# Output projection of an encoder layer as seven block products, with weight sums made in device memory and the second norm in two token halves

## What is computed

```python
mix = jnp.concatenate([o_att, o_hg], axis=-1) @ w_out[l]      # (512 x 2048) @ (2048 x 2048)
x = x + g1 * rms_norm(mix, norm_mix_post[l])
h = rms_norm(x, norm_ffn_pre[l]) * (1.0 + sc2) + sh2
y = conv_glu_ffn(h, w_up[l], conv_w[l], conv_b[l], w_down[l])  # starts with h @ w_up
```

## Time and profile before

| | us |
|---|---|
| median of 3 runs (lowest, highest) | 2378.76 (2375.49, 2380.01) |
| span of the profiled execution, from first to last instruction | 2375.8 |
| busy in it: PE / PEld / DVE / ACT / POOL | 2334.7 / 2025.8 / 1878.8 / 1104.8 / 128.6 |
| mean granted clock of TensorE | 0.997 |

### The profile page before, as it was taken

The page is one execution under the profiler, slowest core; times in us unless marked ns, Lnnn a source line. Parts: engine busy times, 40 slices in busy tenths (PEclk is TensorE's granted clock), DMA queues, the critical chain, the costliest instruction groups (busy, mean ns, idle before and its releaser), DMA issues.

```text
span 2375.8 us, 37218 instructions
## 1 busy us (share of the span) xinstructions
PE 2334.7 (98%) x13671; PEld 2025.8 (85%) x13671; DVE 1878.8 (79%) x2447; ACT 1104.8 (47%) x1517; POOL 128.6 (5%) x207
## 2 busy tenths in 40 slices
PE   6999999999999999999999999999999999999998
PEld 3577778888888877878999999999999998888887
DVE  5875667887777873267799999999999998888777
ACT  4266744334443353254444444444444445555554
POOL 1010000000000000000000000000000000001100
PEclk9999999999999999999999999999999999999999
DMA  9952456666666734336555555555555559779966
GB/s 366 346 157 85 133 180 208 215 219 212 207 211 198 234 89 169 98 124 159 146 140 146 145 144 143 144 142 139 141 145 145 142 176 329 251 207 285 279 226 224
DMA packets 378834, 442.47 MB, mean 186 GB/s; under 512 B 14876, under 2 KB 295716, under 8 KB 376448
## 3 DMA queue, kind: packets, MB, share of 16 engines
q1 hardware_dynamic: 359056, 369.74, 49.1%
q0 software_dynamic: 19696, 71.68, 13.0%
HBM read 418.81 MB, written 66.08 MB: 204 GB/s over the span
## 4 chain that ended last, share of the span: by engine, by line
PE 87%; DVE 5%; DMA 3%; ACT 2%; issue 2%; SPq 0%; DVEq 0%; ACTq 0%
PE bank L2132 26%; PE bank L2134 26%; PE bank L2133 26%; DMA ADA<-in_w_ada_dram 2%; PE bank L2295 2%; DVE ACC L1373 2%; DMA AB_raw<-in_w_ada_dram 1%; PE bank L2198 1%; DVE ZZ L1577 1%; PE bank L2375 1%; PE bank L2314 1%; PE bank L2189 1%; DVE W_lo L1332 0%; PE bank L2063 0%; DVE AB_acc L1636 0%
## 5 line engine op out<-in xcount | busy, mean ns | idle before, releaser
L2132 PE MATMUL bank<-H_lo,W_hi 128*128 128x256 f32 (+1 forms) x1832 | 635.7, 347 | 0.0
L2134 PE MATMUL bank<-H_hi,W_lo 128*128 128x256 f32 (+1 forms) x1832 | 613.6, 335 | 0.0
L2133 PE MATMUL bank<-H_hi,W_hi 128*128 128x256 f32 (+1 forms) x1832 | 613.2, 335 | 0.0
L2132 PEld LDWEIGHTS bank<-H_lo,W_hi 128*128 128x128 f32 x1832 | 349.3, 191 | 35.8 <-issue 6.2
L2133 PEld LDWEIGHTS bank<-H_hi,W_hi 128*128 128x128 f32 x1832 | 349.3, 191 | 35.7 <-issue 6.2
L2134 PEld LDWEIGHTS bank<-H_hi,W_lo 128*128 128x128 f32 x1832 | 348.8, 190 | 35.6
L2132 PE MATMUL bank<-T_lo,W_hi 128*128 128x256 f32 x1280 | 362.2, 283 | 0.0
L2133 PE MATMUL bank<-MGR,W_hi 128*128 128x256 f32 x1280 | 362.2, 283 | 0.0
L2134 PE MATMUL bank<-MGR,W_lo 128*128 128x256 f32 x1280 | 362.2, 283 | 0.0
L2132 PEld LDWEIGHTS bank<-T_lo,W_hi 128*128 128x128 f32 x1280 | 245.8, 192 | 0.0
L2133 PEld LDWEIGHTS bank<-MGR,W_hi 128*128 128x128 f32 x1280 | 245.8, 192 | 0.0
(11 more groups left out here) (311 smaller groups left out, 3741.7 us busy)
## 6 DMA issues: line engine op xcount, KB each, us to landing
AB_raw<-in_w_ada_dram SPq DMA_DIRECT2D x128, 512.0 KB, 4.4
UB<-in_w_up_dram SPq DMA_DIRECT2D x100, 512.0 KB, 4.1
W_raw<-in_w_in_dram SPq DMA_DIRECT2D x90, 512.0 KB, 4.8
t_dram<-in_w_down_dram POOLq DMA_DIRECT2D x88, 512.0 KB, 8.1
DRAW<-in_w_down_dram SPq DMA_DIRECT2D x66, 512.0 KB, 5.8
W_raw<-in_w_up_dram SPq DMA_DIRECT2D x56, 512.0 KB, 3.9
ADA<-in_w_ada_dram SPq DMA_DIRECT2D x48, 512.0 KB, 9.0
W_raw<-in_w_down_dram SPq DMA_DIRECT2D x44, 512.0 KB, 6.1
```

The source lines that it names most:

```text
L2132: pe.matmul(acc, st_hi, mv_lo, start=start, stop=False, skip_group_check=on)
L2133: pe.matmul(acc, st_hi, mv_hi, start=False, stop=False, skip_group_check=on)
L2134: return pe.matmul(acc, st_lo, mv_hi, start=False, stop=stop, skip_group_check=on)
```

## The change

**Seven products.** The projection is computed in 2 x 2 blocks: the 512 tokens in two halves, the 2048 rows of `w_out` in two halves of 1024, its columns in two halves of 1024. Seven products of (256 tokens x 1024) by (1024 x 1024) take the place of eight. Each has 8 units (128 rows of a weight or weight sum by 1024 columns), so there are 56 units of four steps (two token tiles by two column halves), 224 steps in all. The order is the list `OUT`. Four products need sums or differences of blocks of `MX`: DVE makes them in place (`combine`), and the parts go to `CH` and `CL` (four slots each of 8 rows by 256 tokens). Four banks (`CHAIN_A`) carry products 1, 6, 5, 3, 2 on top of each other, four (`CHAIN_C`) 7, 4 and, after a copy of product 1 back into them, 2; ACT keeps states (`keep_chain`), DVE adds them.

**Weight sums.** The products 7, 6, 5 and 4 use sums of blocks of `w_out`. POOL makes them in device memory (`out_sum`, 56 transfers of 512 KB): 16 copies beside the rotations of attention, 16 adds, 8 copies and 8 adds beside the heads, one for every two units, and 8 adds after `GROW` is loaded. SP waits for the last 8 ahead of product 4. The 22 copies of `w_down` move from the heads into the loop over the channel sub-layer (`sum_t2`, three for every two tiles).

**Last head.** `OUT_STEPS` now leaves out 4 of the first 56 steps instead of 8; 60 steps (15 units) lie in the last head. The gates are transposed at step 71.

**Norm in halves.** The right token half (tiles 2 and 3) is done after product 3, and its norm, its transposes (`turn_h2`, 16 turns of two transposes) and its splits lie beside product 2. The 30 matmuls without use go. `up_row` runs 16 times for the right half and 16 times for the left (256 columns each instead of 512).

```diff
+OUT = ([(1, k) for k in range(8)] + [(6, k) for k in range(7)] + [(7, 0), (6, 7), (7, 1)] + [(5, k) for k in range(8)]
+       + [(7, k) for k in range(2, 8)] + [(3, 0), (3, 1)] + [(4, k) for k in range(8)] + [(3, k) for k in range(2, 8)]
+       + [(2, k) for k in range(8)])
+OUT_PLACES = [(0, 1, 2)[v % 3] if v < 9 else (3, 4, 0, 1, 2)[(v - 9) % 5] for v in range(len(OUT))]
...
-        OUT_STEPS = [g for g in range(56) if g not in (23, 29, 35, 41, 47, 52, 53, 54)] + [57, 60, 65, 70, 73, 75, 77, 79]
+        OUT_STEPS = [g for g in range(56) if g not in (35, 41, 47, 53)] + [57, 60, 65, 70, 73, 75, 77, 79]
-        ROW_LAG = 2
+        ROW_LAG = 4
-        SEAM_STEPS = 30
...
             def load_out(v):
+                if product == 4 and k == 0:
+                    sp.wait_ge(o6_landed, o6_count + 4 * 8 * 16)
...
+            def out_sum(n):
+                phase, k = n // 8, n % 8
+                if phase == 0:
+                    pool.dma_start(o6_dram[k], w_out[0, top, 0:1024]).then_inc(o6_landed, 16)
...
+                else:
+                    pool.wait_ge(o6_landed, o6_count + 3 * 8 * 16)
+                    pool.wait_ge(lo_ready, U_OUT + OUT_END[6])
+                    pool.dma_start(o6_dram[k], w_out[0, low, 0:1024], accum_op=ALU.add).then_inc(o6_landed, 16)
...
+                out_sum(2 * n)
+                out_sum(2 * n + 1)
...
+            for n in range(16, 48):
+                pool.wait_ge(unit_used, U_HG + 10 + (n - 16) * 2)
+                out_sum(n)
...
+            MIX_LO_AT = {7: 2, 14: 3, 18: 4, 23: 5, 28: 6, 40: 7}
+            COMBINE_AT = {9: 3, 15: 4, 19: 5, 24: 6, 34: 7}
             for g in range(STEPS):
...
+                if g in OUT_STEPS and OUT_STEPS.index(g) % 4 == 2:
+                    split_lo_out(OUT_STEPS.index(g) // 4 + LEAD)
...
+                if v == OUT_END[7]:
+                    dve.wait_ge(unit_used, U_OUT + OUT_END[7])
+                    dve.wait_ge(chain_kept, 12)
+                    for b in range(4):
+                        dve.tensor_tensor(mg_block(b, 1), bank, Y_V[:, b // 2, blk], ALU.add).then_inc(chain_added, 1)
+                        dve.tensor_tensor(bank, bank, Y_U[:, b // 2, blk], ALU.add).then_inc(chain_added, 1)
...
+                if v == 42:
+                    dve.wait_ge(unit_used, U_OUT + OUT_END[4])
+                    for b in range(4):
+                        gate_bank(CHAIN_C[b], 2 + b // 2, b % 2)
+                    sum_mix(0, 6)
+                    sum_mix(1, 8)
+                    make_x1(0, 4)
+                if v == 43:
+                    make_x1(1, 6)
...
+                if v == 48:
+                    dve.wait_ge(unit_used, U_OUT + OUT_END[3])
+                    for b in (2, 3, 0, 1):
+                        gate_bank(CHAIN_A[b], b // 2, 2 + b % 2)
+                if v + LEAD < len(OUT):
+                    split_lo_out(v + LEAD)
...
+            sum_mix(2, 14)
+            h2_low(14)
+            make_x1(2, 12)
+            dve.wait_ge(unit_used, U_OUT + len(OUT))
+            for b in (2, 3):
+                dve.wait_ge(mg_squared, 12 + b + 1)
+                gate_bank(CHAIN_C[b], 1, b - 2)
+            sum_mix(3, 16)
             split_lo(0, 4, U_UP + 2)
+            make_x1(3, 14)
+            split_lo(0, 4, U_UP + 3)
+            scale_x1(2)
+            h2_low(15)
+            scale_x1(3)
...
+            for n in range(KT):
+                up_row(n)
+            pe.wait_ge(mg_ready, 14)
+            pe.wait_ge(mg_squared, 16)
+            for n in range(KT, 2 * KT, 2):
+                turn_h2(n)
+                turn_h2(n + 1)
+                if n >= KT + ROW_LAG:
+                    up_row(n - ROW_LAG)
+                    up_row(n - ROW_LAG + 1)
```

More of the change, by code:

```diff
@@ L396, in hybrid_encoder_layer, with raw_count, out_source, out_landing @@
         FRONT_Q = [FRONT_ORDER.index(n) + 1 for n in range(FRONT_HEADS)]
-        OUT_BANKS = [[0, 1, 6, 7], [2, 3, 4, 5]]
+        CHAIN_A, CHAIN_C = (0, 1, 6, 7), (2, 3, 4, 5)
         X_BANK = 2
-        SEAM_STEPS = 30
+        def raw_count(k):
+            return (k - FULL) // 2 + 1 - (OUT_NOT_RAW if k >= U_UP else 0)
+        def out_source(product):
+            rows, tokens = {1: (0, left), 7: (0, left), 6: (0, left), 3: (0, left), 5: (0, right),
+                            2: (8, left), 4: (8, right)}[product]
+            return lambda k0, k1: MX[:, rows + k0:rows + k1, tokens]
+        def out_landing(v):
+            place = OUT_PLACES[v]
+            if v < RAW:
+                return raw_landed[v], 16 * raw_count(U_OUT + v)
+            return out_landed[place], ada2_count[place] + 16 * sum(1 for w in range(RAW, v + 1) if OUT_PLACES[w] == place)
+        def mg_block(b, c):
+            return MG[:, b // 2 + (2 if c in (0, 1) else 0), b % 2 * 512 + (1024 if c in (1, 3) else 0):b % 2 * 512 + (1536 if c in (1, 3) else 512)]
         def g_pair(m):
@@ L658, in _ @@
                 store_out(tt)
-            sp.wait_ge(out_stored, 16 * sum(len(out_pieces(tt)) for tt in range(TT)))
+            sp.wait_ge(out_stored, tables_count + 16 * sum(len(out_pieces(tt)) for tt in range(TT)))
         @block.gpsimd
@@ new lines, in _ @@
+            for r in range(2):
+                if r == 0:
+                    act.wait_ge(mix_tile_done, 1)
+                else:
+                    act.wait_ge(unit_used, U_OUT + len(OUT))
+                for b in (2 * r, 2 * r + 1):
+                    out_square(PB[CHAIN_C[b]][:, :], r, b % 2)
+                mix_root(2 + r)
+            split_hi(0, 4, U_UP + 2)
+            x1_norm(2)
+            split_hi(0, 4, U_UP + 3)
+            x1_norm(3)
+            for n in range(KT, 2 * KT):
+                h2_out(n)
+                h2_high(n)
@@ L1726, in _, with gate_bank, sum_mix @@
-            dve.wait_ge(xr_landed, 16 * TT)
-            for tt in range(TT):
-                if tt == TT - 1:
-                    split_lo(0, 4, U_UP)
-                dve.wait_ge(mg_squared, 3 * TT + tt + 1)
+            def gate_bank(bank, tt, cb):
+                dve.tensor_tensor(MG[:, tt, cb * 512:(cb + 1) * 512], PB[bank][:, :], GROW[:, cb * 512:(cb + 1) * 512],
+                                  ALU.mult).then_inc(mg_ready, 1)
+            def sum_mix(n, squared):
+                tt = TILE_ORDER[n]
+                dve.wait_ge(mg_squared, squared)
@@ L1757, in _ @@
+            make_x1(3, 14)
[3 more added lines that the diff above has]
+            scale_x1(3)
+            for n in range(KT, 2 * KT):
+                h2_low(n)
             split_lo(0, 4, U_UP + 4)
@@ L2430, in out_step @@
[L2430 to L2436 removed]
+                    if product in (6, 5, 3):
+                        pe.wait_ge(chain_kept, {6: 0, 5: 4, 3: 8}[product] + b + 1)
@@ new lines, in out_step, with out_banks @@
+                bank = PB[(CHAIN_C if product in (7, 4, 2) else CHAIN_A)[b]]
+                t, w = slice(b // 2 * P, (b // 2 + 1) * P), slice(b % 2 * 512, (b % 2 + 1) * 512)
+                opens = product in (1, 7)
+                return three_passes(bank[:, :], CH[n][:, k, t], CL[n][:, k, t], W_hi[:, slot, w], W_lo[:, slot, w],
+                                    opens and k == 0, opens and k == 7, not opens)
+            def out_banks(v):
+                return (0, 2, 3, 1) if v == 0 else range(4)
@@ new lines, in up_row @@
+            def up_row(n):
+                kt, tokens = H2_ORDER[n % KT], (left if n >= KT else right)
+                pe.wait_ge(h2_lo, n + 1)
+                if n == 0:
+                    pe.wait_ge(mg_ready, 10)
+                    pe.wait_ge(mg_squared, 12)
+                w = slice((kt % 8) * P, (kt % 8 + 1) * P)
+                for half in range(2):
+                    u = U_UP + half + (0 if kt >= 8 else 2)
+                    if n in (0, 8):
+                        pe.wait_ge(lo_ready, u + 1)
+                    ins = three_passes(PB[half][:, tokens], W_hi[:, u % SLOTS, w], W_lo[:, u % SLOTS, w],
+                                       H_hi[:, kt, tokens], H_lo[:, kt, tokens], n % KT == 0, n % KT == KT - 1)
+                    if n >= KT and kt % 8 == 7:
+                        ins.then_inc(unit_used, 1)
```

571 lines of the change are left out of this document (360 added, 211 removed).

## The result

The changed kernel takes **2414.97 us** (median of 4 runs, 2411.75 to 2422.63), the kernel before 2378.55 beside it: a ratio of 1.0157, 95% interval 1.0138 to 1.0176, 36 us slower where 16 us less were forecast. The profiled execution spans 2414.0 us, 38.2 more than before's.

The account below looks back on a forecast made before the run. PE, busy in 98% of the span, was taken to bound the kernel. The terms -21.8 + 3.4 - 0.3 + 5.6 + 3.6 - 10.5 + 4 gave -16.0 us, so 2362.8 us, range 2347 to 2373.

Parts of the forecast that it names:

- 8: Transfers: in the heads, 24 adds and 8 copies replacing 22 copies would cost zero, at worst +4 us.
- The last additions: Projection: the last 8 adds would be done at 943, 5 us to spare, costing 0, at worst +12 us.
- rival C: The last 8 adds run one after the other, PE waits 31 us at v = 34, total 2394 us; chance 0.08.
- 1, fewer matmuls: Projection: 256 steps become 224, saving 96 matmuls at 0.2267 us each, -21.8 us.
- 2, the last head: Last head: DVE's fuller list makes PE wait, +3.4 us, ends 0 and +8.
- 4, waits in the projection: Projection: PE waits for splits queued behind norm work in DVE's ordered list, +5.6 us, ends +1.5 and +8.
- (b): Projection, v = 42: gates, squares, root, `x1` and split take 9.0 us against 5.44, so +3.6 us at v = 44.
- (a): Projection, v = 32: eight bank additions and the split take 6.1 us, so PE waits +0.7 us.
- step 3: Gates transposed inside the last head: PE's 0.7 us wait goes, product 7's third bank waits about 0.4; -0.3 us.
- 6, the seam: Last projection matmul to last row: 30.6 us for 41.1, so -10.5 us with one 3.2 us wait; ends -14.5 and -5.
- 7, the clock: Waits at v = 44 and in the seam each bring a spell at the lower clock, +4 us (0 to +5).
- B: DVE and the adds cost more: head +7, waits +8, adds +4, total 2371 to 2375 us; chance 0.16.

Follow-up runs that it names:

- e1: Changed kernel without the 24 additions and 8 copies beside the heads: 2375.33 us.
- e7: Changed kernel with the same 32 transfers beside the heads issued in bunches of four or five at each head's ninth unit: 2390.93 us.
- e9: Changed kernel in e8's order, 16 copies and 16 additions beside attention, 16 transfers in bunches at the ninth unit of heads 2 to 7: 2368.60 us.
- e10: e9 with a memory block of its own for the fourth sum, 8 more copies and no sum transfers beside the projection: 2369.88 us.
- e2: Changed kernel with the 24 additions beside the heads made plain copies of the same bytes to the same places: 2389.34 us.
- e3: Changed kernel without the last 8 additions beside the projection: 2417.16 us.
- e8: e4 with the splits for steps 44 to 46 ahead of the `x1` work, and the seam's first up-phase units split before the last `x1` rows: 2362.34 us.
- e11: e9 with the `w_down` transfers beside the up projection issued two per stored block instead of one and a half: 2370.92 us.
- e12: e11 with the 32 transfers beside attention spread by the load of the DMA engines: 2363.80 us.
- e4: Changed kernel with no transfers of sums at all, products 4 to 7 reading blocks of `w_out` instead: 2372.38 us.

## Why the prediction was wrong, point by point

**The step that failed is 8, "In the heads ... Zero, at worst +4".** It measured about 40 us (e1). The prediction's own sign of being wrong, "if the heads (340 to 836) get longer, which would be the transfers", came true. The price of an addition was too low, 3.2 us of engine time where I had 2.5; that of a copy was fair, 1.5 for 1.6. The earlier trace rows has nine additions issued but 4.19 MB moved, the bytes of eight, so it gives 2.8. The share rose to 0.72 where I had put 0.75, but over a longer stretch: 0.72 of 537 us is 387 us of engine time, which in the old 496 would be 0.78. That alone doesn't reach one. What failed is the step from a mean share below one to no cost. I named as cover that "PE idles 2.4 us there and the weight loads have two units ahead". The loads that VectorE uses directly, `AB_raw`, had no such lead, and the profile of before said so: 29 waits for them in the heads, 14.3 us. Even `W_raw` was waited for 6 times (9.3 us) in spite of its two units, and 15 times after (30.6). In the chain that ended last on the two pages `AB_raw`'s loads rise from 1% to 5% of the span, those of `W_raw` reach 1%, so most of the loss goes by `AB_raw`; how much by each no run separates. A load that is waited for has no slack left; whatever delays it further goes into VectorE's list, and from there to TensorE as soon as the list's own slack is used up. I also argued that single transfers are easier than the bunches of three copies of before. e7, e9 and e10 show the opposite as long as the bunch fits into a stretch in which the loads rest: up to four additions at a head's end cost at most about 1 us, five cost 4. e2 adds that the copies I counted at nothing cost too when spread over the units (14 us for 32).

**The last additions** (8, "0, at worst +12"): about 3 us (e9 against e10, 2.8; e3 gives 3.0 with the clock in it). In the 40 us behind the last head's output they land after 21.4 us in the median, and a weight load beside them after 11.9, 5.3 in the earlier trace rows. They share with the loads rather than block them, which is what I took from the earlier trace rows, and rival C is out. By the rule of the Trainium skill named there ("DMA: Bandwidth & Descriptors", section "Queues, rings and completion order") the engines alternate between queues that hold work; the trace fits it, 21.4 and 11.9 us side by side. It may also be how an addition hurts a load in the heads, since a queue that gets its turn can still get it late; no run shows the turns themselves.

**1, fewer matmuls:** the instruction count falls by 30, which is 96 + 30 less the 96 of the halved rows, as said. The price held: away from the waits the starts are 0.2267 us apart, and the stretch from the last head's output to T has 487 matmuls on 512 columns for 595 (12 of the 108 are the fillers that moved into the last head).

**2, the last head:** +7.3 for 6.1; TensorE's wait for the merged keys is 2.1 us in one place, as worked out.

**4, waits in the projection:** the working of (b) holds to a tenth. VectorE begins the four gates at 1026.21, `x1` at 1031.81, the split at 1034.08, and TensorE goes on at 1035.35, 9.1 us after the start (9.0):

```profile
1026.21 2.48 DVE L1920 TENSOR_TENSOR MG<-bank,GROW 128x512 f32<-128x512 f32 x4 [3.06 <-PE bank L2398]
...
1031.81 2.35 DVE L1935 SCALAR_TENSOR_TENSOR XR<-MG,SM,XR 128x2048 f32<-128x2048 f32 x1
1034.08 1.22 DVE L1889 TENSOR_TENSOR W_lo<-ORAW,W_hi 128x1024 fp32r<-128x1024 f32 x1
```

```profile
1035.35 0.80 PE L2396 MATMUL bank<-W_lo,CH 128*128 128x512 f32 x1 [3.73 <-DVE W_lo L1889]
```

That is 3.73 us at v = 44 for 3.6, and of (a) 0.66 at v = 34 for 0.7. (The last line of the prediction calls a wait at v = 34 a sign of being wrong, though (a) had forecast one; it isn't the wait for the sums that rival C meant.) What I left out are five small waits of 0.6 to 1.6 us earlier in the list: a factor's low part 1.1, the copy of a bank 0.6, low splits 1.6, 0.6 and 0.7, of which the last two go with the last additions (e3). The 0.8 and 0.5 that I had put at v = 45 and 48 didn't come. Counted from start to start, as what the distances exceed 0.2267 by, the eight waits of the stretch come to 10.5 us where I had 6.0 (0.4 of step 3 and the 5.6). So waits are 4.5 of the 6.4 us by which the projection missed its forecast, the longer spell of the lower clock is 0.8, and about 1 us stays without a place.

**5, transposes:** eight groups of four take 0.35 us each and make the next distance 0.09 longer, 3.5 us for 3.6.

**6, the seam:** I had one wait of 3.2 us; there are two, of 2.36 (1083.28) and 2.91 (1086.79), both for low splits. -6.3 for -8.5. A further 1.1 us is lost between VectorE's fourth and fifth reading of an up-projection bank, 22 to 33 us after the first.

**7, the clock:** right in kind. Behind the wait at v = 44 the matmuls come at 0.43 us for 0.2267, and the granted clock of the stretch is 0.72, the lower level (1.2 of 2.4 GHz) for a part of it; between 1075 and 1112 it is 0.91. From the starts, 13 matmuls took 5.7 us for 2.9 there, and 25 on 256 columns took 5.5 for 3.0 behind 1086.79: 5.3 us for the two spells where I had 4.

```profile
1030.00:1042.00 12.00, 8.27 (x26) 6.22 (x25) 9.95 (x10) 11.92 (x18) 0.53 (x1) 0.72 0.47 157
```

e8, without the wait at v = 44 and with 1.6 us for 5.3 in the seam, has 1.00 in both stretches, so the clock fell because of these waits.

**8, the copies of `w_down` in the up projection** ("zero"): zero for 850 us, in which the two kernels keep their distance to 0.1 us, and then 2.3 us at the start of the down projection, where a third of these copies is still in flight. e11 moves it; the wait goes and the stretch is 1.3 us shorter.

**Of the rivals** none had the result. B had the additions at +4, C had them serial. The rival that was missing is: spread additions delay loads that are already waited for. The share of 0.75 that I had worked out would have had to be read against the 0.67 at which those loads were late already. The other side of it: with the transfers in quiet places the change gives 2363.8 us, near the 2362.8 forecast. That is partly chance, since e12 also has the better order of e8, which the forecast didn't.

**Open:** the 2.5 us that the first head's output is later in e4, which has no sums either (one trace of each kernel; near the start of attention, at TensorE's wait for `Q_lo`, e4 is 1.2 us late already and after 2.7); and whether it is the engines' queues or the memory behind them in which a load waits for an addition. The loads' packets themselves took no longer beside the additions: in the 40 us behind the last head's output SP's queue used 30.6% of the engines for 4.62 MB, 2.65 us a MB, and in e4 47.0% for 6.37 MB, 2.95 us. That speaks for the queues and doesn't prove them.

## What to carry to other kernels

Before transfers are added "beside" a stage, look in the waits for loads that are waited for there already, however shortly: they have no slack, and a mean DMA share of 0.7 says little: it was 0.72 in the slow heads and 0.70 in those of e12. Put the new transfers where the share falls to nothing inside the stage, in bunches that fit there, or into a stage where the engines have idle time; the same 56 transfers of sums cost some 43 us in one placement (after less e4) and 6 in another (e9 less e8). And a piece of norm work in an in-order list belongs behind the next split that TensorE needs, not ahead of it.

## What the runs showed of the hardware

An addition in memory of 512 KB took 3.2 us of all 16 engines beside the heads and landed after 7.9 us, a copy 1.5 and 4.5. With eight additions queued, one landed after 21.4 us and loads beside them after 11 to 12. Cutting the additions in half, with the same bytes, halved the longest wait of a load (4.5 to 2.3 us). The copies beside the heads, which I had taken as free, cost 14 us for 32 when spread evenly (e2). Four additions in a row at a head's end cost at most about 1 us (e7, e10), five in a row 4 us (e7).
